# Gated DeltaNet's head norm, gating and output product as one stage

## The reference, cut to what matters

```python
o = chunk_gated_delta_rule(q, k, v, g, beta)
o = rms_norm(o, w_norm) * jax.nn.silu(z.reshape(b, t, GDN_V_HEADS, GDN_HEAD_DIM))
return o.reshape(b, t, GDN_V_DIM).astype(h.dtype) @ w_out
```

## Time and profile before

| | |
|---|---|
| median of 3 runs | 2056.11 us (2055.52 to 2057.75) |
| the profiled execution | 2057.27 us |
| its span, first to last instruction | 2055.5 us |
| mean granted TensorE clock | 0.972 |
| TensorE busy | 1907.9 us (93%) |
| VectorE, ScalarE, GpSimd busy | 1072.4, 857.5, 172.0 us |
| the back stage | some 354 to 537.2 us |
| the head norm | 537.5 to 563.0 us |
| the output product | 563.4 to 676.0 us |

### The profile page before, as it was taken

How to read it: one execution, slowest core, us unless ns; L and a number is a source line. 1 busy time by engine, 2 the same in 40 slices (tenths; PEclk the granted TensorE clock), 3 DMA queues, 4 the chain that set the end, 5 groups by cost and what they waited for, 6 DMA issues and landing times. The chain is left out here.

```text
span 2055.5 us, 31449 instructions
## 1 busy us (share of the span) xinstructions
PE 1907.9 (93%) x12756; PEld 1704.2 (83%) x12756; DVE 1072.4 (52%) x1754; ACT 857.5 (42%) x1375; POOL 172.0 (8%) x188
## 2 busy tenths in 40 slices
PE   7999998889779999999989977999999998899988
PEld 6999998779579999999989955778888885787666
DVE  6666577875663343444452266544444346852243
ACT  5557743445552433333233244443323334334342
POOL 0001230222400000000000021000000002000101
PEclk9999999999989999999999999999999999999999
DMA  7223452222172222232223221233232222421101
GB/s 172 86 88 120 125 161 65 52 66 71 28 183 83 83 95 91 82 102 82 94 59 96 72 60 57 82 103 96 89 102 84 99 82 64 124 62 42 42 1 41
DMA packets 206173, 173.91 MB, mean 85 GB/s; under 512 B 42160, under 2 KB 181424, under 8 KB 206056
## 3 DMA queue, kind: packets, MB, share of 16 engines
q1 hardware_dynamic: 206056, 172.27, 28.1%
HBM read 161.40 MB, written 10.83 MB: 84 GB/s over the span
## 5 line engine op out<-in xcount | busy, mean ns | idle before, releaser
L163 DVE TENSOR_TENSOR main_wlo<-raw,main_whi 128x2048 fp32r<-128x2048 f32 x106 | 242.9, 2292 | 365.7 <-ACT main_whi L156 365.7
L156 ACT CAST main_whi<-raw 128x2048 fp32r<-128x2048 f32 x106 | 201.6, 1903 | 411.9 <-PE ps L178 410.6
L178 PE MATMUL ps<-ffn_xhi,main_whi 128*128 128x264 f32 (+1 forms) x768 | 206.3, 323 | 6.6 <-DVE ffn_xlo L648 6.6
L178 PE MATMUL ps<-ffn_xhi,main_wlo 128*128 128x264 f32 (+1 forms) x768 | 206.6, 324 | 0.0
L178 PE MATMUL ps<-ffn_xlo,main_whi 128*128 128x264 f32 (+1 forms) x768 | 206.4, 323 | 0.0
L178 PE MATMUL ps<-ffn_ahi,main_wlo 128*128 128x264 f32 (+1 forms) x768 | 205.2, 322 | 0.0
L178 PE MATMUL ps<-ffn_alo,main_whi 128*128 128x264 f32 (+1 forms) x768 | 205.0, 321 | 0.0
L178 PE MATMUL ps<-ffn_ahi,main_whi 128*128 128x264 f32 (+1 forms) x768 | 203.9, 320 | 0.0
L178 PE MATMUL ps<-gdn_xhi,gdnf_whi 128*128 128x264 f32 x768 | 163.4, 294 | 8.1 <-DVE gdn_xlo L519 4.4
L178 PE MATMUL ps<-gdn_xlo,gdnf_whi 128*128 128x264 f32 x768 | 158.3, 288 | 0.0
L178 PE MATMUL ps<-gdn_xhi,gdnf_wlo 128*128 128x264 f32 x768 | 158.0, 287 | 0.0
(11 more groups left out here) (500 smaller groups left out, 3767.9 us busy)
## 6 DMA issues: line engine op xcount, KB each, us to landing
raw<-in_ff_up_dram SPq DMA_DIRECT2D x32, 1024.0 KB, 5.4
raw<-in_ff_down_dram SPq DMA_DIRECT2D x32, 1024.0 KB, 5.0
raw<-in_gdn_in_dram SPq DMA_DIRECT2D x24, 1024.0 KB, 5.6
raw<-in_w_in_dram SPq DMA_DIRECT2D x14, 1024.0 KB, 5.2
raw<-in_mlstm_in_dram SPq DMA_DIRECT2D x12, 1024.0 KB, 5.4
raw<-in_gdn_out_dram SPq DMA_DIRECT2D x8, 1024.0 KB, 7.3
gdn_v_spilled<-gdn_o SPq DMA_DIRECT2D x16, 264.0 KB, 2.2
gdn_z_spilled<-gdn_o SPq DMA_DIRECT2D x16, 264.0 KB, 2.7
```

Of the source, the lines that this page charges most:

```text
L156: k.nc.scalar.copy(k.whi[:, slot % SPLIT_SLOTS, :], k.raw[:, slot, :]).then_inc(k.hi_done, 1)
L163: eng.tensor_tensor(k.wlo[:, s, :], k.raw[:, slot, :], k.whi[:, s, :].bitcast(F32), ALU.subtract).then_inc(k.lo_done, 1)
L178: mm = pe.matmul(ps[:, b, 0:k.width], w, x[:, half], start=first and n == 0, stop=last and n == 2)
```

## The change

The two stages `head_norm` and `gated_down` become one, `normed_down`. SiLU and the multiplication by `w_norm` are put on the gates before that: on 8 of them (`ORDER[:8]`, the gates 0 and 9 to 15) in the front, where they leave PSUM, and on the other 8 (gates 1 to 8) in the back, which loads them from DRAM into a new tile `gate`, works on them in ScalarE's last three busy slots and stores them again. The heads are taken in the order `ORDER` = 0, 9 to 15, 1 to 8. Unit 1's products run 6 heads behind unit 0's (`BEHIND`).

```diff
+LATE = 8
+ORDER = [0, *range(1 + LATE, GV), *range(1, 1 + LATE)]
 # FrontTiles.act, tile j >= 32
-            k.nc.scalar.copy(two(self.o[:, s % 2, :]), halves(k.ps[b])).then_inc(self.copied, 1)
+            gate = j - self.tiles
+            if gate not in ORDER[:GV - LATE]:
+                k.nc.scalar.copy(two(self.o[:, s % 2, :]), halves(k.ps[b])).then_inc(self.copied, 1)
+                return
+            k.nc.scalar.activation(two(self.o[:, s % 2, :]), halves(k.ps[b]), ACT.Silu).then_inc(self.gated, 1)
+            act.wait_ge(self.gain_in, 16)
+            act.wait_ge(self.gated, ORDER.index(gate) + 1)
+            k.nc.scalar.activation(self.o[:, s % 2, :], self.o[:, s % 2, :], ACT.Copy, scale=self.gain[:, 0:1])\
+                .then_inc(self.copied, 1)
 # gdn_back, SP
+                if u < LATE:
+                    sp.dma_start(gate[:, u, :], k.z_d.ap()[ORDER[GV - LATE + u]]).then_inc(s.gate_in, 16)
...
+            for i in range(LATE):
+                sp.wait_ge(s.gate_done, i + 1)
+                sp.dma_start(k.z_d.ap()[ORDER[GV - LATE + i]], gate[:, i, :]).then_inc(s.gate_stored, 16)
+            sp.wait_ge(s.gate_stored, 16 * LATE)
 # gdn_back, ScalarE, at the end of a slot
+            def gates(first, last):
+                act.wait_ge(s.gate_in, 16 * LATE)
+                for i in range(first, last):
+                    nc.scalar.activation(gate[:, i, :], gate[:, i, :], ACT.Silu).then_inc(s.gated, 1)
+                for i in range(first, last):
+                    act.wait_ge(s.gated, i + 1)
+                    nc.scalar.activation(gate[:, i, :], gate[:, i, :], ACT.Copy, scale=gain[:, 0:1]).then_inc(s.gate_done, 1)
+                if NU <= t < NU + 3:
+                    gates((0, 2, 5)[t - NU], (2, 5, LATE)[t - NU])
 # normed_down, SP
+            for i in range(kts):
+                if i == 4:
+                    for u in range(loaded, RAW_SLOTS):
+                        load_unit(k, sp, u0 + u, cols(u), ring(u))
+                if i >= 4:
+                    sp.wait_ge(scaled, i - 3)
+                sp.dma_start(gate[:, i % 4, :], gate_d.ap()[ORDER[i]]).then_inc(gate_in[i % 4], 16)
 # normed_down, GpSimd
+            for i in range(kts):
+                if i >= 3:
+                    pool.wait_ge(summed, i - 2)
+                pool.tensor_tensor(sq[:, i % 3, :], head(i), head(i), ALU.mult).then_inc(squared, 1)
 # normed_down, ScalarE
+            def logarithm(i):
+                act.wait_ge(summed, i + 1)
+                if i >= 3:
+                    act.wait_ge(scaled, i - 2)
+                nc.scalar.activation(two(rinv[:, i % 3, :]), halves(k.ps[2 + i % 2]), ACT.Ln, scale=1.0 / P,
+                                     bias=k.eps[:, :]).then_inc(log, 1)
+            def root(i):
+                act.wait_ge(log, i + 1)
+                nc.scalar.activation(rinv[:, i % 3, :], rinv[:, i % 3, :], ACT.Exp, scale=-0.5).then_inc(inv, 1)
+            nc.scalar.preload_act_table_set("natural_log_exp_and_others")
             split_hi(k, act, u0, ring(0), t0)
+            logarithm(0)
+            root(0)
             split_hi(k, act, u0 + 1, ring(1), t0)
+            logarithm(1)
+            root(1)
+            for i in range(kts):
+                if i + 2 < kts:
+                    logarithm(i + 2)
+                act.wait_ge(scaled, i + 1)
+                nc.scalar.copy(hi(i), a[:, i % 2, :]).then_inc(hi_ready, 1)
+                if i + 2 < kts:
+                    root(i + 2)
 # normed_down, VectorE
+            def low(i):
+                dve.wait_ge(hi_ready, i + 1)
+                dve.tensor_tensor(lo(i), a[:, i % 2, :], hi(i).bitcast(F32), ALU.subtract).then_inc(lo_ready, 1)
             split_lo(k, dve, u0, ring(0))
+            for i in range(kts):
+                dve.wait_ge(inv, i + 1)
+                dve.tensor_tensor(rinv[:, i % 3, :], rinv[:, i % 3, :], head(i), ALU.mult).then_inc(normed, 1)
+                if i > 0:
+                    low(i - 1)
+                if i == 2:
+                    split_lo(k, dve, u0 + 1, ring(1))
+                dve.wait_ge(normed, i + 1)
+                dve.wait_ge(gate_in[i % 4], 16 * (i // 4) + 16)
+                if i >= 2:
+                    dve.wait_ge(lo_ready, i - 1)
+                dve.tensor_tensor(a[:, i % 2, :], rinv[:, i % 3, :], gate[:, i % 4, :], ALU.mult).then_inc(scaled, 1)
 # normed_down, TensorE
+            def total(i):
+                pe.wait_ge(squared, i + 1)
+                if i >= 2:
+                    pe.wait_ge(log, i - 1)
+                for hf, half in enumerate(HALVES):
+                    mm = pe.matmul(k.ps[2 + i % 2][:, hf, 0:HT], k.ones[:, :], sq[:, i % 3, half], start=True, stop=True)
+                mm.then_inc(summed, 1)
+            total(0)
+            total(1)
+            pe.wait_ge(k.lo_done, u0 + 1)
+            for i in range(kts):
+                if i + 2 < kts:
+                    total(i + 2)
+                pe.wait_ge(lo_ready, i + 1)
+                one(0, i)
+                if i == BEHIND:
+                    pe.wait_ge(k.lo_done, u0 + 2)
+                if i >= BEHIND:
+                    one(1, i - BEHIND)
+            for i in range(kts - BEHIND, kts):
+                one(1, i)
+            pe.wait_ge(log, kts)
```

More of the change, by code:

```diff
@@ L844, in dve_end @@
         pass
[L847 to L920, removed]
@@ L1800, in gdn_back @@
         below = sb("below", [P, CH])
+        gate = sb("gate", [P, LATE, T])
         vf = sb("vf", [P, VFS, GRP, CH])
@@ L2248, in gated_down @@
         ahi, alo = sb("ahi", [P, kts, T], F32R), sb("alo", [P, kts, T], F32R)
-        hi = lambda kt: ahi[:, kt, :]
-        lo = lambda kt: alo[:, kt, :]
-        z, a = sb("z", [P, 3, T]), sb("a", [P, 2, T])
-        z_in = [k.sem(f"{name}_z{j}") for j in range(3)]
-        gated, scaled, hi_ready, lo_ready, added = (k.sem(f"{name}_{x}") for x in (
-            "gated", "scaled", "a_hi", "a_lo", "added"))
+        sq, rinv, a, gate = sb("sq", [P, 3, T]), sb("rinv", [P, 3, T]), sb("a", [P, 2, T]), sb("z", [P, 4, T])
+        hi = lambda i: ahi[:, i, :]
+        lo = lambda i: alo[:, i, :]
+        head = lambda i: value(ORDER[i])
+        gate_in = [k.sem(f"{name}_z{j}") for j in range(4)]
+        squared, summed, log, inv, normed, scaled, hi_ready, lo_ready, added = (k.sem(f"{name}_{x}") for x in (
+            "squared", "summed", "log", "inv", "normed", "scaled", "a_hi", "a_lo", "added"))
         tail = NextSums(name)
@@ L2261, in _ @@
         def _(sp):
-            for u in range(loaded, RAW_SLOTS):
-                load_unit(k, sp, u0 + u, cols(u), ring(u))
-            for kt in range(kts):
-                if kt >= 3:
-                    sp.wait_ge(scaled, kt - 2)
-                sp.dma_start(z[:, kt % 3, :], gate_d.ap()[kt]).then_inc(z_in[kt % 3], 16)
+            for i in range(kts):
[5 more added lines that the diff above has]
+                sp.dma_start(gate[:, i % 4, :], gate_d.ap()[ORDER[i]]).then_inc(gate_in[i % 4], 16)
             for u in range(RAW_SLOTS, n):
@@ L2274, in _ @@
             sp.wait_ge(k.gains_in, 16 * len(later_gains))
+        @block.gpsimd
+        def _(pool):
+            for i in range(kts):
+                if i >= 3:
+                    pool.wait_ge(summed, i - 2)
+                pool.tensor_tensor(sq[:, i % 3, :], head(i), head(i), ALU.mult).then_inc(squared, 1)
         @block.scalar
         def _(act):
+            def logarithm(i):
[8 more added lines that the diff above has]
+            nc.scalar.preload_act_table_set("natural_log_exp_and_others")
             split_hi(k, act, u0, ring(0), t0)
+            logarithm(0)
+            root(0)
             split_hi(k, act, u0 + 1, ring(1), t0)
[L2280 to L2287 removed]
+            logarithm(1)
[7 more added lines that the diff above has]
+                    root(i + 2)
             for u in range(n):
@@ L2320, in _, with one @@
         def _(pe):
-            def one(u, kt):
-                s = ring(u) % SPLIT_SLOTS
+            def total(i):
[5 more added lines that the diff above has]
+                mm.then_inc(summed, 1)
+            def one(u, i):
+                s, kt = ring(u) % SPLIT_SLOTS, ORDER[i]
                 whi = k.whi[:, s, :].rearrange("p (k n) -> p k n", k=kts)
                 wlo = k.wlo[:, s, :].rearrange("p (k n) -> p k n", k=kts)
-                mm = product(k, pe, k.ps[u % 4], whi[:, kt, :], wlo[:, kt, :], hi(kt), lo(kt), kt == 0, kt == kts - 1)
-                if kt == kts - 1:
+                mm = product(k, pe, k.ps[u % 4], whi[:, kt, :], wlo[:, kt, :], hi(i), lo(i), i == 0, i == kts - 1)
+                if i == kts - 1:
                     mm.then_inc(k.tile_full, 1)
-            pe.wait_ge(k.lo_done, u0 + 2)
-            for kt in range(kts):
-                pe.wait_ge(lo_ready, kt + 1)
-                one(0, kt)
-                one(1, kt)
+            total(0)
[13 more added lines that the diff above has]
+            pe.wait_ge(log, kts)
```

(4 more changed lines are left out.)

46 lines of the change are left out of this document (14 added, 32 removed).

## The result

The changed kernel takes 2093.14 us (median of 4 runs, 2085.3 to 2095.37), the kernel before 2055.82 us beside it (4 runs, 2053.84 to 2057.75): ratio 1.0173, interval 1.0159 to 1.0187, so 37.3 us slower. The forecast was 2085, with a range of 2069 to 2099. The profiled execution took 2091.71 us, its span 2089.8.

The account below looks back on a forecast made before the run. TensorE was taken as busy nearly everywhere, its products the floor, with idle stretches and cold products to gain. 0.75 + 3.0 - 25.1 + 55.5 - 5.5 gave +28.7 us, 2084.8, range 2069 to 2099.

Parts of the forecast that it names:

- The ring: Joint stage: product(i-1), sum(i+2), logarithm(i+2), cast(i), low part(i), product(i) form a closed cycle, nothing overlapping, for 13 rounds.
- Front, +0.75: Front's gates 0 and 9 to 15: Silu and scaling replace a copy; only the last tile ends the stage, +0.75 us.
- Back, +3.0: Back's eight gates on ScalarE in the last three slots, plus the last store's landing: +3.0 us, ends 0.4 and 14.
- Start, first product 10 us in: Joint stage's start: first output product after 10 us where it took 35.15, so -25.1 us.
- The rounds, 71.4: Joint stage's 13 rounds: 58.7 us at upper clock, 84.1 at lower; middle 71.4; all heads 81.7 against 26.2, +55.5.
- After the heads, -5.5 and no gap at unit 2: Unit 2 onward: the 3.64 us gap and the cold restart go, -5.5 us; 576 products take 70.3.
- The sum: Whole kernel: 0.75 + 3.0 - 25.1 + 55.5 - 5.5 = +28.7 us, 2084.8.
- A (clock full): Rival: same ring in the joint stage, clock stays full; +16.0 us, 2072.1; chance 0.22.
- B (half clock): Rival: same ring in the joint stage, clock stays at half; +41.4 us, 2097.5; chance 0.14.
- C (no ring): Rival: sums run ahead of low parts in the joint stage, so no ring closes; -11.0 us, 2045.1; chance 0.09.
- D (back in full): Rival: the back's gate activations and landing push the whole tail, 14 us for 3.0; +39.7, 2095.8; chance 0.08.

Follow-up runs that it names:

- two different cuts: Changed kernel with ScalarE's cast of head i ahead of logarithm i+2 (2054.36 us, 0.9994), or with TensorE's sums one head further ahead (2051.47 us, 0.9977).
- held: Changed kernel with ScalarE casting first, SP's gate-store wait moved into the joint stage, and GpSimd's square i waiting for low part i-3: 2050.19 us, 0.9970.
- no_back_gates: Against `both`: loads, activations and stores of gates 1 to 8 left out of the back; 2048.04 us, 0.9953 of the kernel before.
- landed: Against `both`: SP's wait for the gate stores moved from the back's end to its first load in the joint stage; 2049.92 us, 0.9962.
- the second execution: The changed kernel run and traced again with no edit: 2090.93 us, ratio 1.0161 to the kernel before.
- both: Changed kernel with ScalarE's cast ahead of the logarithm and TensorE's sums one head further ahead: 2051.95 us, 0.9973 of the kernel before.
- unit1_later: Against `both`: weight unit 1's cast on ScalarE moved behind the first round; 2050.96 us, 0.9963 of the kernel before.
- tuned6: `both` plus late landing, unit 1's cast later, six late gates, and the front's last weight casts ahead of the tile's Silu: 2049.56 us, 0.9958.

## Why the prediction was right, and where it was off

- *The ring decides, and the result is slower.* Right: two different cuts each take away 39 to 42 us (37 and 40 by the ratios), 33 to 34 of them in the stage of the traces, and the waits turn 13 times.
- *Front, +0.75.* Silu and scaling behind the last tile take 1.43 us where the copy took 0.60, so the step's +0.83 is there, but the stage's end does not show it: it lies between 352.06 and 355.08 us in the seven traces with this front and back, in the mean at 353.1, and at 353.10 and 353.22 in the two of the kernel before. The +1.98 of the first trace (353.10 to 355.08) is scatter in the main. TensorE's wait of 3.6 us for a unit's low part is none of the change's doing: it is 3.7 in the kernel before, and its subtraction (323.76, before 323.59) starts ahead of the last unit's cast (323.91, before 322.75). The Silu out of PSUM took 0.61 us, not 0.70.
- *Back, +3.0.* The tail costs 1.9 (15.32 against 13.43), nearly all of it the landing, as the step said ("the last store must land"); its activations are hidden but for 0.1. Front and back together came to 3.7 in the means of 7 and 2 traces, where the sum had 3.75, but that agreement is luck in part: 1.9 are the tail, the front shows nothing, and the other 1.8 lie inside the back, ahead of the gates. That stretch, from the front's end to the last but one copy of new values, took 171.0 and 169.0 us in the kernel before and 170.9 to 172.3 in the seven; no run here tells the difference from scatter.
- *Start, first product 10 us in.* 10.66, twice. I put nothing down for GpSimd's early squares beyond 0.4. In the changed kernel two ways were equally long: ScalarE's third logarithm started 7.74 us in (forecast 7.5) and ended at 551.18, and VectorE had head 0 ready at 551.23. The 0.66 us over the forecast are VectorE's next operation, 1.57 us beside a square, which the low part stood behind. With the cast ahead of the logarithm only VectorE's way is left, and the squares then cost 1.75 us (held); what holding them back would give in the changed kernel's own order was not run.
- *The rounds, 71.4.* 69.6 in the first execution (553.40 to 623.02). Both levels of the mean are now measured: 3.94 and 4.68 us at full clock (forecast 4.12 and 4.85), 5.50 and 6.82 at the lower (forecast 5.74 and 7.09; the logarithms at 571.77 and 577.27 of the first trace, and the rows above). The mean was right for the first trace by luck of the draw: in the second the rounds take 7 us more.
- *After the heads, -5.5 and no gap at unit 2.* Right: 634.59 to 705.06 is 70.5 us, forecast 70.3.
- *The sum.* In the joint stage -25.1 + 55.5 - 5.5 = +24.9 stands against +25.1 in the first pair of traces and +32.8 in the second (169.50 against 136.71). The term that was mis-sized is the ring's, where it took the clock half way between its levels: from the first product to unit 0's add it is 65.71 us with the gaps filled, 76.07 in the first execution and 83.22 in the second, so the clock's share is 10.4 and 17.5 us where the sum had 12.7. With 3.7 ahead of it the two executions come to +28.8 and +36.5; the medians are +37.3 and +34.9. Of the first trace's rest, 3.9 us lie behind the stage, where every kernel scatters (1379.7 to 1387.4 us). The first batch's +37.3 is not accounted for in full: the two longest runs (2094.57 and 2095.37) were not traced. The nine runs of this kernel do go nearly in the order of their mean granted clock over the whole program, from 0.967 and 0.965 (2084.39 and 2085.3 us) to 0.958, 0.955 and 0.958 (2094.57, 2094.68 and 2095.37), but that does not say in which stage it was lost.
- *The rivals.* A (clock full): the stage with filled gaps is 14.8 us over the kernel before (152.00 against 137.22) where A had 12.2, its clock being low in the first rounds (mean 0.81 from 551.60 to 562.00, 0.97 from there to 612.00); but unfilled, the clock falls, as the earlier trace rows had it. B (half clock): true of six rounds in one execution. What the prediction held against it, that TensorE's 60% or more of busy time might bring the clock up again, did not happen there: TensorE stood still in 2.06 of 6.82 us, round after round, and the clock stayed at 0.50. C (no ring): with both cuts the stage is 9.4 us under the kernel before (127.78) where C had 14.8; 1.5 us of the difference are the first product (11.53 us in, forecast 10), and 4.3 the first six rounds (550.29 to 569.49, 19.2 us where C had 14.9), in which VectorE has operations of 1.5 us. D (back in full): out, by no_back_gates and landed.

The Trainium skill (TensorE: Matmul & The Clock Gate, "A second HAM failure mode: psum-queue depth-cycling") tells of a kernel whose short idle moments between groups of matmuls made the clock swing between its two levels. The trace agrees: idle times of 2.05 us in a round, mean clock 0.75 and, over the same window of the second execution, 0.62. The Trainium skill's rule beside rival A (same page, "Why this matters for your kernels"), taken to mean that shorter gaps are safe, would have kept the clock up, and the measurement decides against that.

## What to carry to other kernels

When stages are joined, write down each engine's queue in its order and follow one item through all of them: if item i+2 of one engine stands behind item i-1 of another and ahead of item i of a third, the sum of all the links is the time of a round, however idle the engines are. Cut such a ring at one place, by moving one instruction; either of the two places tried here did nearly all, and a second cut brought little. Price the round at both clocks, for a ring leaves TensorE gaps, and with them its clock fell here, and give the range for both, not their mean.

## What the hardware showed that I had not expected

*VectorE and GpSimd take turns.* The prediction read slow squares beside slow products as sharing. The timeline of `both`, GpSimd between VectorE's operations, fits turns better:

```profile
562.96 0.70 DVE L2287 TENSOR_TENSOR gdn_out_a<-gdn_out_rinv,gdn_out_z 128x528 f32<-128x528 f32 x1
563.62 1.54 DVE L2278 TENSOR_TENSOR gdn_out_rinv<-gdn_out_rinv,wide 128x528 f32<-128x528 f32 x1
565.08 0.70 DVE L2274 TENSOR_TENSOR gdn_out_alo<-gdn_out_a,gdn_out_ahi 128x528 fp32r<-128x528 f32 x1
...
563.04 1.55 POOL L2236 TENSOR_TENSOR gdn_out_sq<-wide 128x528 f32<-128x528 f32 x1 [2.59 <-PE ps L2304]
```

The square starts at 563.04, inside an operation that ends at 563.66, and ends at 564.59, 0.93 us after it (alone it takes 1.07). VectorE's next, started at 563.62, ends at 565.16, 0.57 us after the square. Each one's time is the rest of the other's and then most of its own. The Trainium skill (SBUF — State Buffer, "SBUF: two separate sides") has it so, an exclusive lock for a whole instruction; this trace agrees.

*One program, two lengths of a stage.* In the rounds at 1.2 GHz of the second execution TensorE stood still for 2.06 us of 6.82 and its clock did not rise. In the first, with the same queues, it rose and fell again: it fell while TensorE worked, and was up again behind an idle time of 2.06 us. Windows of that trace (columns as before), the idle time being 604.15 to 606.21:

```profile
600.25:601.15 0.90, 0.90 (x7) 0.90 (x8) 0.90 (x2) 0.00 (x0) 0.00 (x0) 1.00 0.00 0
601.35:604.15 2.80, 2.80 (x9) 1.85 (x8) 0.05 (x1) 0.00 (x0) 0.00 (x0) 0.50 0.36 97
606.25:607.75 1.50, 1.50 (x12) 1.50 (x13) 1.14 (x2) 0.00 (x0) 0.00 (x0) 1.00 0.00 0
```

The stage's length was a matter of the execution, by 7 us (162.32 and 169.50). With the ring opened by both cuts five different kernels, one trace each, lie within 1.1 us: `unit1_later` 127.47, `no_back_gates` 127.51, `landed` 127.53, `both` 127.78 and `tuned6` 128.53.
